# Mixer B of a two-block transformer kernel: probabilities turned and copied head by head in one PSUM bank, the values of a pair alone in the other, made in the middle of a step

## What is computed

```python
def nsa_attention(h, w_in, w_out, cmp_pos, cmp_w1, cmp_w2, rel_table):
    G, R, dh = B_KV_GROUPS, N_HEADS // B_KV_GROUPS, HEAD_DIM      # 4 groups, 4 heads each, 64
    q, kc, vc, ks, vs, kw, vw, gate = jnp.split(h @ w_in, splits, axis=-1)
    ...
    o_cmp = jnp.einsum("bgrsn,bngd->bsgrd", p_cmp.astype(vc_b.dtype), vc_b)
    ...
    o_slc = selected_block_attention(q, to_kv(ks), to_kv(vs), sel_idx, rel_table)
    o_win = banded_attention(q.reshape(B, S, N_HEADS, dh), to_kv(kw), to_kv(vw), rel_table, B_WINDOW)
    g = jax.nn.sigmoid(gate.astype(jnp.float32)).reshape(B, S, N_HEADS, 3).astype(o_win.dtype)
    o = (g[..., 0:1] * o_cmp.reshape(B, S, N_HEADS, dh) + g[..., 1:2] * o_slc + g[..., 2:3] * o_win)
    return o.reshape(B, S, -1) @ w_out
```

## Time and profile before

| What | Value |
|---|---|
| median of 3 runs | 2666.72 us (2665.9 to 2670.82) |
| profiled execution, its own time | 2666.94 us |
| its span in the trace | 2664.7 us |
| granted TensorE clock, mean | 0.994 |
| PE busy | 2594.8 us, 97% |
| DVE, ACT, POOL busy | 68%, 54%, 7% |
| chain that ended last | PE 86%, DVE 5%, ACT 3%, DMA 2% |
| steps 28 to 44 of mixer B | 1441.5 to 1514.3 us of the span |

### The profile page before, as it was taken

One profiled execution on the slowest core, in us unless ns is written; L12 is line 12 of the kernel. 1 busy time (PEld: TensorE's weight loads), 2 busy tenths in 40 slices (PEclk: granted clock), 3 DMA queues, 4 the chain that ended last, 5 costly groups with the idle time before them and its releaser, 6 DMA issues.

```text
span 2664.7 us, 43984 instructions
## 1 busy us (share of the span) xinstructions
PE 2594.8 (97%) x15457; PEld 2259.9 (85%) x15457; DVE 1808.8 (68%) x2578; ACT 1449.8 (54%) x2304; POOL 189.1 (7%) x266
## 2 busy tenths in 40 slices
PE   7999999999999999999989999999999999999999
PEld 7888888888888878888888688888888888888887
DVE  6866668666766676676676666676656667666766
ACT  4655546455555565555555655555556555555654
POOL 2010001000000030000001200000010000002000
PEclk9999999999999999999999999999999999999999
DMA  6559845487566447656654266566446666653664
GB/s 188 160 171 236 226 152 159 143 238 210 170 194 189 137 148 219 190 177 195 190 175 134 88 200 190 178 196 189 151 138 194 189 205 181 199 164 129 184 191 144
DMA packets 587098, 473.78 MB, mean 178 GB/s; under 512 B 19676, under 2 KB 546416, under 8 KB 586480
## 3 DMA queue, kind: packets, MB, share of 16 engines
q1 hardware_dynamic: 582768, 457.37, 56.6%
q0 software_dynamic: 3312, 14.36, 2.4%
q10 hardware_dynamic: 912, 0.63, 0.1%
HBM read 469.09 MB, written 6.37 MB: 178 GB/s over the span
## 4 chain that ended last, share of the span: by engine, by line
PE 86%; DVE 5%; ACT 3%; DMA 2%; issue 2%; POOL 1%; DVEq 1%; SPq 0%; POOLq 0%; ACTq 0%
PE acc L784 20%; PE gu L751 14%; PE tp L751 14%; PE tp L758 7%; PE gu L758 7%; PE acc L817 3%; DVE lo_a L454 2%; ACT hi_a L442 1%; DMA raw_a<-in_w_in 1%; PE acc L1463 1%; PE gu L1421 1%; PE gu L1430 1%; PE acc L1465 1%; PE acc L1464 1%; PE gu L1422 1%
## 5 line engine op out<-in xcount | busy, mean ns | idle before, releaser
L454 DVE TENSOR_TENSOR lo_a<-raw_a,hi_a 128x2048 fp32r<-128x2048 f32 (+1 forms) x313 | 711.1, 2272 | 359.1 <-ACT hi_a L442 357.7
L442 ACT ACTIVATE hi_a<-raw_a 128x2048 fp32r<-128x2048 f32 (+1 forms) x313 | 591.5, 1890 | 125.2 <-PE acc L1465 31.7
L751 PE MATMUL tp<-xT,hi_a 128*128 128x512 f32 x1600 | 398.4, 391 | 0.0
L751 PE MATMUL gu<-xT,hi_a 128*128 128x512 f32 x1600 | 397.9, 391 | 0.0
L751 PEld LDWEIGHTS gu<-xT,hi_a 128*128 128x128 f32 x1600 | 294.0, 188 | 56.9
L751 PEld LDWEIGHTS tp<-xT,hi_a 128*128 128x128 f32 x1600 | 293.4, 188 | 56.4
L784 PE MATMUL acc<-hi_b,h_hi 128*128 128x512 f32 x760 | 298.6, 393 | 1.3 <-issue 1.2
L784 PE MATMUL acc<-lo_b,h_hi 128*128 128x512 f32 x760 | 297.9, 392 | 0.0
L784 PE MATMUL acc<-hi_b,h_lo 128*128 128x512 f32 x760 | 295.7, 389 | 0.0
L466 DVE TENSOR_TENSOR lo_b<-raw_b,hi_b 128x1024 fp32r<-128x1024 f32 x210 | 255.9, 1219 | 0.0
L843 ACT ACTIVATE arena<-arena 128x256 f32<-128x256 f32 x200 | 83.6, 418 | 279.0 <-DVE arena L906 279.0
(11 more groups left out here) (344 smaller groups left out, 4100.8 us busy)
## 6 DMA issues: line engine op xcount, KB each, us to landing
raw_a<-in_ffn_w_in SPq DMA_DIRECT2D x352, 512.0 KB, 5.8
raw_b<-in_ffn_w_out SPq DMA_DIRECT2D x176, 512.0 KB, 3.7
raw_a<-in_w_in SPq DMA_DIRECT2D x52, 512.0 KB, 4.7
raw_a<-in_w_gate SPq DMA_DIRECT2D x44, 512.0 KB, 5.6
raw_a<-in_w_up SPq DMA_DIRECT2D x44, 512.0 KB, 6.8
raw_b<-in_w_down SPq DMA_DIRECT2D x44, 512.0 KB, 4.7
raw_a<-in_w_out SPq DMA_DIRECT2D x24, 512.0 KB, 4.3
raw_a<-in_c_w_in SPq DMA_DIRECT2D x24, 512.0 KB, 4.4
```

The source lines that it names most:

```text
L442: nc.scalar.activation(a_view(hi_a, par)[:, :, 0:width], a_view(raw_a, par)[:, :, 0:width], ACT.Copy).then_inc(a_hi, 1)
L454: nc.vector.tensor_tensor(a_view(lo_a, par)[:, :, 0:width], a_view(raw_a, par)[:, :, 0:width], a_view(hi_a, par)[:, :, 0:width].bitcast(F3 ...
L751: nc.tensor.matmul(banks[:, e, :], w_hi[:, kt, e * P:(e + 1) * P], xT[:, :, kt, :], start=(kt == 0), stop=False)
```

## The change

In mixer B alone, a unit is now turned one head at a time. `turn_head_pe` transposes the three 128-column blocks of one head into columns 0 to 383 of bank 0; `turned_head_act` copies these 384 columns, and the second head may be transposed only when the first copy is done (`head_out`), since it goes to the same columns. The pair's values keep columns 256 to 511 of bank 1, which nothing else now uses, so neither turn nor copy waits for `o_lo`; the values product does. On PE the values move from the end of an even step to its middle, ahead of the turn; in odd steps head 0 is turned in the middle and head 1 at the end; in even steps both stand at the end. On ACT a unit's second copy comes first in a step, the values' high part one step earlier and behind the exponentials, and the first copy behind that. `probT` holds the columns in the new order.

```diff
-            if s.kind == "B":
-                pe.wait_ge(cmp_pt_out, 2)
-                if w >= 3:
-                    pe.wait_ge(o_lo, s.pair0 + (w - 1) // 2)
-            elif w >= 1:
+            if w >= 1:
                 pe.wait_ge(o_lo, s.pair0 + w)
...
+        def turn_head_pe(pe, s, w, hh):
+
+            g = s.unit0 + w
+            if hh:
+                pe.wait_ge(head_out, w + 1)
+            else:
+                pe.wait_ge(prob_ready, g + 1)
+                pe.wait_ge(pt_act, g)
+                pe.wait_ge(cmp_pt_out, 2)
+            for k in range(3):
+                mm = nc.tensor.transpose(tp[:, 0, k * P:(k + 1) * P], probs[g % 3][:, hh, k * P:(k + 1) * P], ident)
+            mm.then_inc(pt_whole if hh else head_turned, 1)
+
+        def turned_head_act(act, s, w, hh):
+
+            g = s.unit0 + w
+            if hh:
+                act.wait_ge(pt_whole, g + 1)
+            else:
+                act.wait_ge(head_turned, w + 1)
+            nc.scalar.activation(probT[:, g % 2, hh * 384:(hh + 1) * 384], tp[:, 0, 0:384], ACT.Copy)\
+                .then_inc(pt_act if hh else head_out, 1)
...
             pe.wait_ge(pt_act, g + 1)
+            if s.kind == "B" and w >= 3:
+                pe.wait_ge(o_lo, s.pair0 + w // 2)
...
+            if s.kind == "B":
+                if scored(s, p - 3) is not None and scored(s, p - 3) % 2:
+                    woven_values_pe(pe, s, scored(s, p - 3))
+                elif scored(s, p - 2) is not None:
+                    turn_head_pe(pe, s, scored(s, p - 2), 0)
...
-            if scored(s, p - 2) is not None:
+            if scored(s, p - 2) is not None and s.kind != "B":
                 woven_turn_pe(pe, s, scored(s, p - 2))
...
-                if scored(s, p - 3) is not None and scored(s, p - 3) % 2:
-                    woven_values_pe(pe, s, scored(s, p - 3))
                 compress_pe(pe, s, p)
+                if scored(s, p - 2) is not None:
+                    if scored(s, p - 3) is not None and scored(s, p - 3) % 2:
+                        turn_head_pe(pe, s, scored(s, p - 2), 0)
+                    turn_head_pe(pe, s, scored(s, p - 2), 1)
...
-                if scored(s, p - 4) is not None and scored(s, p - 4) % 2:
-                    values_act(act, s, scored(s, p - 4) // 2)
-                if scored(s, p - 3) is not None and p % 2 == 0:
-                    turned_act(act, s, scored(s, p - 3))
+                if scored(s, p - 3) is not None:
+                    turned_head_act(act, s, scored(s, p - 3), 1)
...
-                if scored(s, p - 3) is not None and p % 2:
-                    if p > 29:
-                        act.wait_ge(o_lo, s.pair0 + (p - 31) // 2 + 1)
-                    turned_act(act, s, scored(s, p - 3))
+                if scored(s, p - 3) is not None and scored(s, p - 3) % 2:
+                    values_act(act, s, scored(s, p - 3) // 2)
+                if scored(s, p - 2) is not None:
+                    turned_head_act(act, s, scored(s, p - 2), 0)
                 ahead_b(hi_slot_a, act, s, p)
```

More of the change, by code:

```diff
@@ L351, in build_block @@
         score_taken = sem("score_taken")
+        head_turned, head_out = sem("head_turned"), sem("head_out")
         score_ready, soft_ready, exp_ready, rden_ready, prob_ready = sem("score_ready"), sem("soft_ready"), sem("exp_ready"), sem("rden_ready"), sem("prob_ready")
@@ L1335, in woven_values_pe @@
                         cols_t = slice(512 + hh * P, 512 + (hh + 1) * P) if t else slice(hh * 256, (hh + 1) * 256)
+                        if s.kind == "B":
+                            cols_t = slice(hh * 384 + 256, (hh + 1) * 384) if t else slice(hh * 384, hh * 384 + 256)
                         mm = nc.tensor.matmul(tp[r, 1, 256 + t * P:512], v[:, t, c:c + HD], probs_t[:, cols_t],
```

## The result

The changed kernel takes 2674.15 us (median of 13 runs, 2671.13 to 2676.34). The kernel before, measured beside it, takes 2669.64 us (13 runs, 2665.9 to 2672.07). The ratio is 1.002, with a 95% interval of 1.0013 to 1.0028: slower by 3.5 to 7.5 us. I had said 2670 us, +3.3 us, and most likely no difference above 0.2%. The sign was right, the size was too small.

A forecast was written before the change was run, and what follows sets the result against it. PE, busy 97% of the span, was taken to bound the kernel. Bare trips and added waits, less removed waits, instructions and half clock, gave +3.3 us, less 0.1 in the tail: 2666.94 + 3.2 = 2670.1, said as 2670 us, range 2666 to 2674.5.

The forecast's parts named there:

- The trips: PE waiting for ACT's copy between a unit's two heads: nine bare round trips, 0.70 us idle each, +6.3 us.
- The 2.31, the 0.95 and the 1.82 us: PE's waits ahead of units 3, 14 and 15 for a late 768-column copy, to be removed: -5.1 us.
- The first fall goes if the 2.31 us gap goes: -1.6.: PE's half clock from the turn of unit 3 was to vanish with the wait ahead of it: -1.6 us.
- the late fall: PE's half clock behind step 43 was to stay, with more idle time ahead of it: +0.1 us.
- one of my signs of being wrong: Wrong if a trip idles PE under 0.5 us, the pair stays at 8.6 us, or the clock falls in other places.
- the clock falls at the early end as well: Rival: idle time between 1452.6 and 1457.3 still brings half clock, +1.6 us, 2671.7 us; chance 0.18.
- The instructions: PE's transposes in 32 head groups, 0.25 or 0.42 us each: 11.1 us against 11.7 before, -0.6 us.
- units 9 and 11: Their head 0, asked for in mid-step, was to wait 0.56 and 0.39 us for POOL: +0.95 us.
- At unit 3: Its head 0, asked for in mid-step, was to wait for POOL until 1456.05, PE free at 1454.6: about +1.5 us.
- heads wait for POOL in every odd step: Rival, steps 33 to 43: each odd step loses more; at 0.6 us each +3.6, 2673.7 us; chance 0.14.
- Trips hidden: Rival: PE starts head 1 as soon as ACT is through, -6.3 us, 2663.8 us; chance 0.08.
- the clock never falls here: Rival: no half clock in this part of the kernel, +1.7 us in all, 2668.4 us; chance 0.09.

The follow-up runs named there:

- the experiment with sixteen: Changed kernel with both heads of every unit turned at the end of the step, so sixteen bare trips instead of nine: 2679.14 us, ratio 1.0036.
- after again: The changed kernel unaltered, profiled once more: one execution of 2674.9 us.
- the spare-place version: Changed kernel with a third place for the first head of every second even unit, turned ahead of the values in even steps: 2674.37 us, ratio 1.002.
- before filled: The kernel before with unused products, eight in the 2.31 us wait of step 31 and six in the 1.82 us wait of step 43: 2666.91 us, ratio 0.9994.
- after filled: The changed kernel with unused products ahead of heads of units 3, 14 and 15: 2673.89 us, ratio 1.0016.
- the reciprocals' version: after filled, with DVE's reciprocals of units 9 and 11 ahead of its scaling of units 10 and 12: one execution, 2674.2 us.
- the last one: before filled, with unit 14 turned into the banks of the scores and seven unused products, not six, ahead of unit 15: 2666.84 us, ratio 0.9989.

## Why the prediction was right, and where it failed

**Right: the mechanism and its price.** The trips were to cost 1.12 us from start to start and be nine: they are 1.13 and nine, and the experiment with sixteen repeats the price. The copy is 0.49 us. The 1.12 is in part luck: ACT starts 0.58 us behind the first transpose (said 0.53), and PE goes on 0.06 us behind the copy (said 0.10), in the trip from 1456.59 to 1457.72. The values behind unit 13 wait 0.78 (said 0.70). The 2.31, the 0.95 and the 1.82 us are gone. Unit 15 waits 1.13 (said 1.3). Pairs from unit 4 on take 8.95, 9.46, 9.46 and 9.39 us (said 9.2 to 9.5).

**Failed: "The first fall goes if the 2.31 us gap goes: -1.6."** This term was worked out as if a fall were the property of a gap. The gap went, and the fall came all the same in one execution of two, behind waits of 0.50, 0.58, 0.95, 0.58 and 0.33 us; and the late fall, which I took as sure in both kernels, stayed away in one of two executions of before. The clock fell in another place than behind step 43, which was one of my signs of being wrong. In the profiled pair the output half of step 33 starts 22.48 us behind the scores of unit 2, 1.59 later than in before, where I had said no later; in after again, without the early fall, it is 21.13. At an equal number of falls the clock adds nothing to the difference, so nothing measured supports a term of -1.6; whether the falls became rarer is open. I had the right case among the rivals (the clock falls at the early end as well, +1.6, 2671.7), with rows that said that such gaps decide by chance, and gave it 0.18.

Without this term the sum is 3.3 + 1.6 = 4.9 us, and the table has 5.35 to 5.51.

**Mis-sized.** What is left, some 0.5 us, is sizes. The instructions were to give 0.6 us back and gave next to nothing: a head group in front of an output product takes 0.30 us and not 0.25 (1486.08 to 1486.38), about 0.55 over the 11 such groups behind unit 3. The scores wait for DVE 0.8 us in two places (said 0.4 in one), while the second head of unit 14 waits no longer than the others (said 0.15 longer): 0.25 more. The values are 0.08 more. Against that, units 9 and 11 wait 0.37 and 0.36 (said 0.95 together), and unit 15 is 0.17 less: 0.39 less in all. Together this is +0.5.

**Missing, and without effect:** the wait of 0.50 us for slot 14. I checked the moved values for what covers their copy, and not for whether their own operand is there. At unit 3 I said a wait of 1.5 us, and it is 0.95 or 0.76: PE comes 0.5 us later, and POOL is done when I said. I had its head at 1456.05, 14.5 us behind the scores of unit 2; it starts 14.58 behind them.

**The range.** Its high end, 2674.6, is 1 us above its own terms: 3.3 + 1.6 + 1.0 + 1.0 = 6.9 over 2666.7 make 2673.6. The upper bound of the copy, 0.60, is half the way from 0.39 to 0.81 and not three quarters.

**The rivals.** That heads wait for POOL in every odd step did not happen: four waits, 2.8 us, of which 0.73 in the middle. But the spare-place version shows that the chain is too long at five units once the trips are covered. Trips hidden: no. That the clock never falls here was seen in no unaltered execution of either kernel, but one fall less was.

What else lies between the two spans stands ahead of the stretch, 3.96 us (behind it after is 0.2 us shorter). The 1.50 us of half clock among them follow the wait for a DMA ahead of unit 1, which before has too (1.76 us, after 1.77) without a fall. In all ten profiles this wait is there, with 1.73 to 1.78 us, and the clock fell behind it in five, one of them a version of before. So that is the chance of the executions profiled. Where the 2.46 us ahead of it come from was not followed up.

## What to carry to other kernels

Splitting one wait into a handover and a shorter wait pays only where other work of the waiting engine stands between the halves: count the places where nothing does, at the start-to-start time of a round trip (here 1.13 us for 0.42 us of work), before counting the long wait as won. Compare two executions in a stretch that holds the change, at an equal number of falls of the clock, since the spans carry falls from elsewhere. When a group is moved ahead, ask of each of its operands who makes it and when: a covered trip may only uncover the chain behind it. And before a new wait is added to the sum, see whether a later wait for something else takes it up, as POOL does here at unit 3.

## What the runs showed of the hardware

The clock of TensorE is not decided by the gap alone. The same kernel held 2.4 GHz or dropped to 1.2 GHz behind the same or nearly the same waits: before at its late end (0.50 in one execution, 1.00 in another, behind 0.95 and 1.82 us), after at its early end (0.50 and 1.00, behind waits of at most 0.95 us). Behind the DMA wait of 1.73 to 1.78 us ahead of unit 1 it fell in five profiles of ten. A fall costs 1.3 to 1.6 us of PE's time. Unused products in the waits kept it at 1.00 at both ends in four executions of four (before filled, after filled, the reciprocals' version and the last one); in the six executions without them it fell at 9 of 12 ends. They cost nothing measurable there: the turn of unit 3 starts 14.83 us behind the scores of unit 2 in before filled, 14.81 in before.

What a group of fp32 transposes costs depends on what stands behind it: three take 0.30 us in front of an output product (1486.08 to 1486.38) and 0.42 in front of scores (1472.14 to 1472.56, both in after); six take 0.57 in front of a projection product and 0.75 in front of scores.
